# Two-block transformer kernel, odd layer: where the query and key norms and rotations are computed

## The chip, the cores and the metric

The kernel runs on one core of one Trainium2 chip. The metric is the device time in microseconds from one launch to its end; lower is better. The kernel before takes 3747.55 us, the median of 3 runs (3745.74 to 3749.96).

## The reference, cut to what matters

Two blocks of two layers each work on one sequence of 512 tokens with 1024 features, in float32. The change lies in the second layer of the second block (the odd layer). Its mixer is grouped-query attention with 16 query heads, 4 key heads and 64 features a head; every head of queries and keys is normed and then rotated.

```python
def odd_mixer(x, w_in, gqa_q_norm, gqa_k_norm, cos_c, sin_c):
    b, s, _ = x.shape
    g = GQA_HEADS // GQA_KV_HEADS
    q, k, v = _split(x @ w_in, ODD_SPLITS)          # 1024, 256, 256 columns
    q = rms_norm(q.reshape(b, s, GQA_HEADS, GQA_HEAD_DIM), gqa_q_norm)
    k = rms_norm(k.reshape(b, s, GQA_KV_HEADS, GQA_HEAD_DIM), gqa_k_norm)
    v = v.reshape(b, s, GQA_KV_HEADS, GQA_HEAD_DIM)
    q = apply_rope(q, cos_c[:, None, :], sin_c[:, None, :]).reshape(b, s, GQA_KV_HEADS, g, GQA_HEAD_DIM)
    k = apply_rope(k, cos_c[:, None, :], sin_c[:, None, :])
    scale = GQA_HEAD_DIM ** -0.5
    def block(qb):
        sc = jnp.einsum('bqkgd,bskd->bkgqs', qb, k) * scale
        pr = jax.nn.softmax(sc.astype(jnp.float32), axis=-1).astype(v.dtype)
        return jnp.einsum('bkgqs,bskd->bqkgd', pr, v)
```

`rms_norm` divides by the root of the mean square of a head's 64 features (plus 1e-6) and multiplies by a gain per feature. `apply_rope` turns feature j of a head together with feature j + 32.

## The kernel before, in words

The program is a row of stages. `stage` opens a block in which each engine runs its own instruction list; it ends in a barrier of all engines (`all_engine_barrier`, L109). Inside a stage the engines are tied by semaphores alone.

`gemm` (L192) is the stage for all projections. Weights come in tiles of 1 MB through a ring of four slots in SBUF, loaded by SP's queue (L244). Every tile is split into a high part (ScalarE, L321) and a low part (VectorE, L353), two tiles deep, and every output is a row of three products per 128 features (L305): 24 matmuls for an output of 512 columns. Output k lands in PSUM bank k modulo `banks` (8 unless given) and is evacuated by ScalarE (`a`) or VectorE (`v`); output k waits until output k - banks is evacuated. The activations themselves are transposed and split at the start (`lead`, L274, L333, L367). With `side` (made by `beside`) a stage carries other work: `side.pe[k]`, `side.act[k]` and `side.dve[k]` are run by those engines just before output k in their own order, and `sp_after[n]` by SP after the load of tile n. Everything is in order on each engine: work that waits holds what is queued behind it. `prepare_beside` (L1093) is such a side for the first block's layers; its rotations swap halves by small transfers from SBUF to SBUF (L1131, L1132), multiply by the cosine on GpSimd (L1160), by the sine on VectorE (L1140) and add on VectorE (L1145).

`odd_mixer` (L1598) runs four stages. First the projection: four tiles of queries (8 outputs of 128 features, copied to `q`), one of keys (2 outputs; each head is stored twice, so `k` has 4 chunks of 128), one of values (4 outputs); the tables are loaded after the weights (`also`). Then `sums_norm` (L1273): ScalarE squares each of 12 chunks (L1293), TensorE sums the squares per head (L1314), one root and one reciprocal over all 24 heads (L1296, L1301), TensorE spreads the result back over the features (L1321, L1322), VectorE multiplies (L1308). Then `rope` (L807): TensorE swaps halves by a permutation matrix (L819), GpSimd multiplies by the cosine (L826), VectorE multiplies the swapped part by the sine (L837) and adds (L843). Then `attention` (L525).

`attention` works in units of 128 queries of one chunk (two heads) against 512 keys; 8 chunks x 4 units = 32 units. For each unit, in a pipeline some units deep: TensorE's scores (L607), VectorE's maximum of both heads, negated (L748), ScalarE's exponentials with their sums (L690), VectorE's reciprocal of the sums (L756), GpSimd's multiplication of the probabilities (L739), TensorE's transposes (L624), the copy to SBUF by ScalarE (L701) or VectorE (L766), and TensorE's product with the values (L642). The last unit of a chunk closes it: ScalarE (L707) and VectorE (L772) take the output out of PSUM in two parts, and the next chunk's first product waits for that. VectorE's order in a step is: closing, maximum of this unit, reciprocal of the one before, copy of the third before. `attention` serves two other layers too.

## Time and profile before

| what | value |
|---|---|
| median of 3 runs | 3747.55 us |
| profiled execution, its own time | 3756.65 us |
| its span from the first to the last instruction | 3754.8 us |
| TensorE busy with matmuls | 3329.8 us (89%) |
| VectorE / ScalarE / GpSimd busy | 1294.7 / 976.5 / 401.7 us |
| mean granted TensorE clock | 0.943 |

The profile is of one execution. Busy time is the time in which an engine had an instruction under way; the granted clock is a share of TensorE's full speed (1.0 is 2.4 GHz, 0.5 is 1.2 GHz). PE is TensorE, PEld its weight loads, DVE VectorE, ACT ScalarE, POOL GpSimd, SP the engine that issues the transfers; a q behind a name means the queue or sequencer of that engine. The durations of matmuls overlap, since they are pipelined: the step from start to start tells what one costs in a row of them.

### The profile page before, as it was taken

What the parts mean: (1) busy time and instruction counts of PE and PEld (TensorE: products, weight loads), DVE (VectorE), ACT (ScalarE), POOL (GpSimd) and SP (SyncE); (2) the same over time, 40 slices, a digit from 0 to 9 for tenths busy, and PEclk for the clock granted to TensorE, in tenths of its full rate; (3) what the DMA queues carried; (4) which work ended last, traced back from release to release, by engine and by line L of the source; (5) the groups of instructions that cost most, each with busy time, mean ns of one, the idle gap of its engine ahead of it and who ended that gap; (6) DMA issues with size and microseconds to landing.
All of it is one profiled execution on the core that took longest, in us unless ns stands there. A gap on an engine that the chain in (4) does not pass through costs nothing. (4 is left out here: it accounts for less than half of the span.)

```text
span 3754.8 us, 42733 instructions
## 1 busy us (share of the span) xinstructions
PE 3329.8 (89%) x17174; PEld 2288.9 (61%) x17174; DVE 1294.7 (34%) x1709; ACT 976.5 (26%) x1557; POOL 401.7 (11%) x403
## 2 busy tenths in 40 slices
PE   7999899998999899999756769999988787999996
PEld 6875587877876487787644367444436346644442
DVE  4324543333523444242344543111113644311112
ACT  4225333222324414231221431000013343100001
POOL 1005100000104300000000610000000561000000
PEclk9999999999998999999977989999998898999998
DMA  5410223333320014331300123999982101499996
GB/s 154 124 45 1 68 81 99 90 90 80 106 90 23 12 56 135 90 93 42 101 7 14 45 80 120 416 424 424 424 341 80 45 23 58 195 420 424 424 423 289
DMA packets 286517, 587.41 MB, mean 156 GB/s; under 512 B 34666, under 2 KB 228408, under 8 KB 237200
## 3 DMA queue, kind: packets, MB, share of 16 engines
q1 hardware_dynamic: 286352, 585.11, 41.9%
q8 instruction: 115, 1.88, 0.2%
q14 instruction: 50, 0.41, 0.0%
HBM read 581.92 MB, written 2.10 MB: 156 GB/s over the span
## 5 line engine op out<-in xcount | busy, mean ns | idle before, releaser
L2010 PE MATMUL ps<-w_ring,xe 128*64 128x512 f32 x1024 | 232.7, 597 | 6.7 <-PEq L109 5.0
L305 PE MATMUL ps<-h_hi,in_w_hi 128*128 128x512 f32 (+1 forms) x528 | 210.1, 398 | 12.8 <-DVE in_w_lo L353 8.2
L305 PE MATMUL ps<-u_hi,mlp_w_hi 128*128 128x512 f32 x512 | 202.3, 395 | 12.0 <-DVE u_lo L976 12.0
L305 PE MATMUL ps<-h_lo,in_w_hi 128*128 128x512 f32 (+1 forms) x528 | 208.4, 395 | 0.0
L305 PE MATMUL ps<-h_hi,in_w_lo 128*128 128x512 f32 (+1 forms) x528 | 207.8, 394 | 0.0
L353 DVE TENSOR_TENSOR mlp_w_lo<-w_ring,mlp_w_hi 128x2048 fp32r<-128x2048 f32 x64 | 146.7, 2292 | 176.9 <-ACT mlp_w_hi L321 176.9
L305 PE MATMUL ps<-h_hi,mlp_w_hi 128*128 128x512 f32 x512 | 199.3, 389 | 3.0 <-DVE h_lo L367 3.0
L305 PE MATMUL ps<-u_lo,mlp_w_hi 128*128 128x512 f32 x512 | 201.4, 393 | 0.0
L305 PE MATMUL ps<-u_hi,mlp_w_lo 128*128 128x512 f32 x512 | 201.1, 393 | 0.0
L305 PE MATMUL ps<-h_lo,mlp_w_hi 128*128 128x512 f32 x512 | 199.2, 389 | 0.0
L305 PE MATMUL ps<-h_hi,mlp_w_lo 128*128 128x512 f32 x512 | 199.2, 389 | 0.0
L2010 PEld LDWEIGHTS ps<-w_ring,xe 128*64 128x64 f32 x1024 | 71.6, 137 | 136.8 <-issue 136.5
L321 ACT ACTIVATE mlp_w_hi<-w_ring 128x2048 fp32r<-128x2048 f32 x64 | 122.1, 1908 | 113.4 <-PE ps L305 113.4
L2088 DVE SCALAR_TENSOR_TENSOR ye_lo<-ps,g_now,ye_hi 128x1024 fp32r<-128x1024 f32 x16 | 20.5, 1284 | 355.0 <-ACT ye_hi L2055 355.0
L2068 DVE TENSOR_TENSOR x<-x,ps 128x512 f32<-128x512 f32 x128 | 82.9, 685 | 173.6 <-PE ps L1973 173.2
L353 DVE TENSOR_TENSOR in_w_lo<-w_ring,in_w_hi 128x2048 fp32r<-128x2048 f32 (+2 forms) x48 | 89.2, 1858 | 141.8 <-ACT in_w_hi L321 141.6
L2010 PE MATMUL ps<-ex_back,xe 128*64 128x512 f32 x512 | 116.9, 597 | 21.4 <-DMA ex_back<-in_w 21.4
L690 ACT ACTIVATE w_ring<-ps,at_top 128x128 f32<-128x128 f32 (+1 forms) x192 | 99.5, 523 | 126.5 <-DVE at_top L748 126.2
L2010 PE MATMUL ps<-ex_front,xe 128*64 128x512 f32 x512 | 116.9, 597 | 15.7 <-DMA ex_front<-in_w 15.5
L1846 PE MATMUL ps<-sel_now,xs_hi 128*128 128x128 f32 x512 | 123.8, 284 | 0.0
L1846 PE MATMUL ps<-sel_now,xs_lo 128*128 128x128 f32 x512 | 122.8, 282 | 0.0
L305 PEld LDWEIGHTS ps<-h_hi,in_w_hi 128*128 128x128 f32 (+1 forms) x528 | 99.5, 188 | 37.6 <-DVE in_w_lo L353 15.2
(513 smaller groups left out, 7176.0 us busy)
## 6 DMA issues: line engine op xcount, KB each, us to landing
w_ring<-in_w SPq DMA_DIRECT2D x192, 1024.0 KB, 12.8
ex_front<-in_w SPq DMA_DIRECT2D x96, 1024.0 KB, 13.3
ex_back<-in_w SPq DMA_DIRECT2D x96, 1024.0 KB, 13.5
w_ring<-in_w_in SPq DMA_DIRECT2D x32, 1024.0 KB, 6.4
w_ring<-in_w_up SPq DMA_DIRECT2D x32, 1024.0 KB, 5.8
w_ring<-in_w_down SPq DMA_DIRECT2D x32, 1024.0 KB, 5.7
w_ring<-in_cmp_w SPq DMA_DIRECT2D x16, 512.0 KB, 4.2
w_ring<-in_w_out SPq DMA_DIRECT2D x8, 1024.0 KB, 6.4
```

The source lines that it names most:

```text
L305: mm = pe.matmul(ps[0:o.rows, k % banks, 0:o.cols], lhsT, rhs, start=(j == 0), stop=(j == len(o.mm) - 1))
L321: act.activation(w.hi[:, n % SPLITS, 0:used], ring.slots[:, n % RING, 0:used], ACT.Copy).then_inc(s.hi_done, 1)
L353: dve.tensor_tensor(w.lo[:, n % SPLITS, 0:used], ring.slots[:, n % RING, 0:used], w.hi[:, n % SPLITS, 0:used].bitcast(F32), ALU.subtract). ...
L690: act.activation(probs[:, u % (LAG + 1), a, 0:n], ps[:, S_BANK + 2 * (u % 2) + a, 0:n], ACT.Exp, bias=top[:, u % 8, a:a + 1], accum_out=to ...
L1846: mm = pe.matmul(ps[:, bank + j // 4, j % 4 * P:j % 4 * P + P], part[:, t, pairs_of(j)], E.sel_now[:, t, :], start=(t == 0 and part is xs. ...
L2010: mm = pe.matmul(ps[rows, bank + half, :], lhsT, slot(2 * m + a)[:, kk, 512 * half:512 * half + 512], start=(k == 0), stop=(k == DC - 1))
L2068: dve.tensor_tensor(d, d, ps[:, TR_BANK + n % 2, :], ALU.add).then_inc(s.added, 1)
L2088: dve.scalar_tensor_tensor(ye.lo[:, :], ps[:, Y_BANK:Y_BANK + 2, :].rearrange("p b n -> p (b n)"), g_now[:, :], ye.hi[:, :].bitcast(F32), ...
```

## The change

The stages `sums_norm` and `rope` of the odd layer are gone; a side, `heads_beside`, carries their work in the projection stage.

- The key tile comes first (outputs 0 and 1), then the four query tiles (2 to 9), then the values (10 to 13). `banks` is 4 (`HEAD_BANKS`); banks 4 to 7 serve the side.
- Query norms: ScalarE squares each query chunk from PSUM as its evacuation, VectorE writes the chunk times the gain. TensorE sums the squares of each head with the tokens on the partitions: `sq` is the stationary operand and two columns of ones move, 4 matmuls a chunk. After a root and a reciprocal the result `rq` (which carries the 1/8 of the attention's scale) is not multiplied into the queries: it is the column by which ScalarE's exponential scales the scores (`sharp`). The negated maximum is multiplied by the same column, by a new VectorE instruction behind the maximum with a wait on VectorE's own semaphore `peaked`. For the other attentions `sharp` is None and nothing is added.
- Key norms: squares on ScalarE, sums on TensorE in two parts (before outputs 3 and 4), root, reciprocal, four transposes (before output 5), split in high and low part, spread back by TensorE in two parts (before 6 and 7), multiplied by VectorE in two parts.
- Rotations: halves are swapped by transfers from SBUF to SBUF issued by SP after the last weight load, four for each chunk with 32 partitions each, in the order queries 0-1, 2-3, keys 0-1, queries 4-5, keys 2-3, queries 6-7. Cosine, sine and sum are all on VectorE. The sine table carries the sign.
- The tables are loaded after weight tile 1, before tiles 2 to 5.

```diff
-                    for a in range(2):
-                        act.activation(probs[...], ps[...], ACT.Exp,
-                                       bias=top[:, u % 8, a:a + 1], accum_out=total[:, u % 8, a:a + 1]).then_inc(s.exped, 1)
+                                       bias=top[:, u % 8, a:a + 1], accum_out=total[:, u % 8, a:a + 1],
+                                       scale=groups[g].sharp(i)[:, a:a + 1] if groups[g].sharp else 1.0).then_inc(s.exped, 1)
...
-                    dve.tensor_reduce(top[:, u % 8, :], ps[:, b:b + 2, 0:keys(i)], AX.X, ALU.max, negate=True).then_inc(s.maxed, 1)
+                    peak = dve.tensor_reduce(top[:, u % 8, :], ps[:, b:b + 2, 0:keys(i)], AX.X, ALU.max, negate=True)
+                    if groups[g].sharp:
+                        peak.then_inc(s.peaked, 1)
+                        dve.wait_ge(s.peaked, u + 1)
+                        peak = dve.tensor_tensor(top[:, u % 8, :], top[:, u % 8, :], groups[g].sharp(i), ALU.mult)
+                    peak.then_inc(s.maxed, 1)
...
-                gemm(nc, "oi", ps, ring, tiles, lead=flips(C, lambda i, j: x[:, i, j * P:(j + 1) * P], h), also=tables)
-        with ExitStack() as c2:
-            chunks = [q[:, j, :] for j in range(8)] + [k[:, j, :] for j in range(4)]
-            sums_norm(nc, "on", ps, C, [(c, gains[:, (n >= 8):(n >= 8) + 1]) for n, c in enumerate(chunks)], add, back[:, :, :])
-            rope(nc, "ro", ps, [(c, cos, sin) for c in chunks], perm)
+                gemm(nc, "oi", ps, ring, tiles, lead=flips(C, lambda i, j: x[:, i, j * P:(j + 1) * P], h), side=side, banks=HEAD_BANKS)
...
+def heads_beside(nc, ctx, ps, C, I, q, k, rq):
...
+    turning = [(q[:, 0:2, :], 0), (q[:, 2:4, :], 1), (k[:, 0:2, :], None), (q[:, 4:6, :], 2), (k[:, 2:4, :], None), (q[:, 6:8, :], 3)]
...
+    def query(c):
+        def a(e, p, st):
+            if c >= 4:
+                e.wait_ge(st.s.n_summed, 1 + (c - 4) // 2 + 1)
+            elif c == 0:
+                e.wait_ge(st.s.n_summed, 1)
+            return e.activation(sq[:, c % 4, :], p, ACT.Square)
+        def v(e, p, st):
+            return e.tensor_scalar(q[:, c, :], p, gains[:, 0:1], None, ALU.mult)
...
+    def swaps(sp, s):
+        for n, (x, g) in enumerate(turning):
+            if g is not None:
+                sp.wait_ge(s.evac_v, s.done_v[Q_OUT + 2 * g + 1])
+            for m in range(x.shape[1]):
+                c = before[n] + m
+                if g is None:
+                    sp.wait_ge(s.n_scaled, m + 1 if n == 2 else m + 3)
+                if c >= 4:
+                    sp.wait_ge(s.n_added, c - 3)
+                for b in (0, 64):
+                    sp.dma_start(tmp[b:b + 32, c % 4, :], x[b + 32:b + 64, m, :]).then_inc(s[f"n_swap{n}"], 16)
+                    sp.dma_start(tmp[b + 32:b + 64, c % 4, :], x[b:b + 32, m, :]).then_inc(s[f"n_swap{n}"], 16)
...
+    def sum_queries(g):
+        def go(pe, s):
+            pe.wait_ge(s.evac_a, s.done_a[Q_OUT + 2 * g + 1])
...
+            for m in (2 * g, 2 * g + 1):
+                for i in range(TT):
+                    mm = pe.matmul(q_sums[g % 2][:, i, 2 * m:2 * m + 2], sq[:, m % 4, i * P:(i + 1) * P], ones[:, 0:2], start=True, stop=True)
+            mm.then_inc(s.n_summed, 1)
...
+    def rotate(n):
...
+            dve.wait_ge(s[f"n_swap{n}"], 64 * len(chunks))
+            for m, c in enumerate(chunks):
+                dve.tensor_tensor(x[:, m, :], x[:, m, :], cos[:, :], ALU.mult).then_inc(s.n_cosined, 1)
+                dve.tensor_tensor(tmp[:, c % 4, :], tmp[:, c % 4, :], sin[:, :], ALU.mult).then_inc(s.n_sined, 1)
+            for m, c in enumerate(chunks):
+                dve.wait_ge(s.n_cosined, c + 1)
+                dve.wait_ge(s.n_sined, c + 1)
+                dve.tensor_tensor(x[:, m, :], x[:, m, :], tmp[:, c % 4, :], ALU.add).then_inc(s.n_added, 1)
...
+    side = beside(names, sp,
+                  {3: sum_keys(0), 4: sum_keys(2), 5: flip_keys, 6: then(spread_keys(0), sum_queries(0)), 7: spread_keys(2), 8: sum_queries(1),
+                   9: sum_queries(2), V_OUT + 1: sum_queries(3)},
+                  {2: square_keys, 4: root_keys, 5: split_hi, 7: root_queries(0), 9: root_queries(1), V_OUT: root_queries(2), V_OUT + 2: root_queries(3)},
+                  {2: tables_in, 4: invert_keys, 5: then(split_lo, rotate(0)), 6: scale_keys(0), 7: then(scale_keys(2), rotate(1)),
+                   8: then(invert_queries(0), rotate(2)), 9: then(invert_queries(1), rotate(3)), V_OUT: then(invert_queries(2), rotate(4)),
+                   V_OUT + 2: rotate(5), V_OUT + 3: invert_queries(3)},
+                  pool, {1: load_tables, 5: swaps})
```

## Rows read from the trace of the kernel before

**Rows 1.** Busy time by stretch: sum (instructions) per engine, clock, DMA share, GB/s

```profile
2840.00:2909.00 69.00, 68.80 (x336) 58.45 (x336) 21.44 (x22) 15.74 (x17) 0.00 (x0) 0.96 0.19 59
2909.00:2938.00 29.00, 21.09 (x48) 10.06 (x48) 13.66 (x16) 9.07 (x14) 0.00 (x0) 0.76 0.00 0
2938.00:2962.00 24.00, 13.50 (x24) 5.56 (x24) 19.94 (x24) 0.00 (x0) 18.89 (x12) 0.71 0.00 1
2962.00:3083.00 121.00, 104.75 (x512) 45.85 (x512) 65.09 (x88) 67.70 (x154) 98.92 (x64) 0.94 0.11 35
...
2962.00:2972.00 10.00, 8.49 (x21) 3.27 (x22) 4.69 (x6) 5.50 (x13) 4.31 (x3) 0.50 0.89 288
```

**Rows 2.** Time line at the stage borders: start, duration (us), engine, line, operation

```profile
2908.84 0.42 DVE L402 TENSOR_SCALAR ov<-ps 128x256 f32<-128x256 f32 x1 [5.33 <-PE ps L305]
...
2910.11 2.19 ACT L1293 ACTIVATE on_sq<-oq 128x512 f32<-128x512 f32 x4 [3.77 <-PEq L109]
...
2962.42 3.78 PE L607 MATMUL ps<-ok,oq 64*128 64x512 f32 x8 [10.23 <-PEq L109]
```

**Rows 3.** Time line of ScalarE inside the projection

```profile
2870.13 0.60 ACT L401 ACTIVATE oq<-ps 128x512 f32<-128x512 f32 x1 [3.46 <-PE ps L305]
2875.63 1.92 ACT L321 ACTIVATE oi_w_hi<-w_ring 128x2048 fp32r<-128x2048 f32 x1 [4.90 <-PE ps L305]
2881.01 0.60 ACT L401 ACTIVATE oq<-ps 128x512 f32<-128x512 f32 x1 [3.46 <-PE ps L305]
```

**Rows 4.** Narrow matmuls of another stage, time line; and a weight load's group

```profile
1068.48 0.55 PE L1189 MATMUL ps<-n_tables,w2k 128*128 128x62 f32 x4
1068.96 0.63 PE L1193 MATMUL ps<-w2v,n_tables 128*31 128x64 f32 x8
1069.53 0.50 PE L305 MATMUL ps<-h_hi,in_w_hi 128*128 128x512 f32 x1
1069.86 0.40 PE L305 MATMUL ps<-h_lo,in_w_hi 128*128 128x512 f32 x1
...
L305 PEld LDWEIGHTS ps<-h_hi,in_w_hi 128*128 128x128 f32 (+1 forms) x528 | 99.5, 188 | 37.6 <-DVE in_w_lo L353 15.2
```

**Rows 5.** VectorE's groups by line: busy us, mean ns, idle before

```profile
L1140 DVE TENSOR_TENSOR gate_a<-gate_a 128x512 f32<-128x512 f32 x16 | 10.3, 684 | 0.0
L1308 DVE SCALAR_TENSOR_TENSOR oq<-oq,gqa_g,ps 128x512 f32<-128x512 f32 x8 | 6.0, 747 | 2.1 <-PE ps L1322 1.3
```

**Rows 6.** Transfers issued by SP, and GpSimd's first use of such a swap

```profile
942.25 0.62 SPq L1131 DMA_DIRECT2D gate_a<-qb  x1
942.92 0.62 SPq L1132 DMA_DIRECT2D gate_a<-qb  x1
...
944.93 1.29 POOL L1160 TENSOR_TENSOR qb<-qb,gate_a 128x512 f32<-128x512 f32 x1 [2.49 <-DMA gate_a<-qb]
...
2852.20 0.43 SPq L248 DMA_DIRECT2D sin<-in_c_sin  x1
```

**Rows 7.** VectorE and GpSimd side by side; one line's duration min/median/max (ns)

```profile
L1232 DVE TENSOR_TENSOR gate_b<-kvc,cpos x16: 565/578/1616, 83.6 to 975.5; 128x248 f32<-128x248 f32 x16
...
967.86 2.29 DVE L353 TENSOR_TENSOR in_w_lo<-w_ring,in_w_hi 128x2048 fp32r<-128x2048 f32 x1 [0.54 <-ACT in_w_hi L321]
...
968.15 4.62 POOL L1160 TENSOR_TENSOR kwd<-kwd,gate_a 128x512 f32<-128x512 f32 x2 [3.61 <-DMA gate_a<-kwd]
```

**Rows 8.** The attention: a wait (total us, times, longest), and GpSimd's time line

```profile
PE ps L642 <- DVE mixT_lo L772: 8.1, 7, 2.0
...
2967.64 46.37 POOL L739 TENSOR_SCALAR gqa_probs<-gqa_probs,gqa_inv 128x512 f32<-128x512 f32 x30 [7.06 <-DVE gqa_inv L756]
```

**Rows 9.** Time line of the attention at the close of a chunk

```profile
3006.63 0.16 DVE L756 RECIPROCAL gqa_inv<-gqa_total 128x2 f32<-128x2 f32 x1
...
3007.40 1.13 PE L607 MATMUL ps<-ok,oq 64*128 64x512 f32 x4
...
3007.51 1.23 DVE L766 COPY gqa_probsT<-ps 128x1024 f32<-128x1024 f32 x1 [0.72 <-PE ps L624]
...
3008.71 0.69 DVE L772 TENSOR_TENSOR mixT_lo<-ps,mixT_hi 128x512 fp32r<-128x512 f32 x1
```

More of the change, by code:

```diff
@@ L1602, in sb @@
             return c.enter_context(nc.sbuf_tensor(name, shape, F32))
-        gains, add, back = sb("gqa_g", [P, 2]), sb("add3", [P, 12, 24]), sb("back3", [24, 12, P])
-        perm, cos, sin = sb("perm3", [P, P]), sb("cos3", [P, T]), sb("sin3", [P, T])
-        gn = [I[n][0].rearrange("(d a) -> d a", a=1) for n in ("gqa_q_norm_2", "gqa_k_norm_2")]
-        tables = ([(gains[64 * m:64 * m + 64, n:n + 1], gn[n]) for m in range(2) for n in range(2)]
-                  + [(add[:, :, :], I["c_add3"]), (back[:, :, :], I["c_back3"]), (perm[:, :], I["c_perm3"]), (cos[:, :], I["c_cos3"]),
-                     (sin[:, :], I["c_sin3"])])
-        q, k, v = sb("oq", [P, 8, T]), sb("ok", [P, 4, T]), sb("ov", [P, TT, 256])
+        q, k, v, rq = sb("oq", [P, 8, T]), sb("ok", [P, 4, T]), sb("ov", [P, TT, 256]), sb("orq", [P, TT, 16])
         with ExitStack() as c2:
             h = pair(nc, c2, "xT_o", [P, DC, T])
-            tiles = [tile(DC, 256, lambda slot, n=n: [(slot, W(w_in, DC, 256 * n, 256))],
-                          lambda w, n=n: [fm(w, h, 128 * j, P, range(DC), **to(q[:, 2 * n + j, :], "AV"[j])) for j in range(2)])
-                     for n in range(4)]
+            side = heads_beside(nc, c2, ps, C, I, q, k, rq)
             def both(dst):
@@ L1624, in both @@
                 return dict(a=a, v=v)
-            tiles.append(tile(DC, 256, lambda slot: [(slot, W(w_in, DC, 1024, 256))],
-                              lambda w: [fm(w, h, 128 * j, P, range(DC), **both(k[:, 2 * j:2 * j + 2, :])) for j in range(2)]))
+            tiles = [tile(DC, 256, lambda slot: [(slot, W(w_in, DC, 1024, 256))],
+                          lambda w: [fm(w, h, 128 * j, P, range(DC), **both(k[:, 2 * j:2 * j + 2, :])) for j in range(2)])]
+            tiles += [tile(DC, 256, lambda slot, n=n: [(slot, W(w_in, DC, 256 * n, 256))],
+                           lambda w, n=n: [fm(w, h, 128 * j, P, range(DC), **side.query(2 * n + j)) for j in range(2)])
+                      for n in range(4)]
             tiles.append(tile(DC, 256, lambda slot: [(slot, W(w_in, DC, 1280, 256))],
@@ L1638, in odd_mixer @@
         groups = [Names(chunk=c, qk=lambda a, c=c: (q[rows(a), c, :], k[rows(a), c // 2, :]),
-                        v=lambda a, kb, c=c: v[:, kb, HD * (c // 2):HD * (c // 2) + HD], bias=None, gate=None, cmp=None) for c in range(8)]
+                        v=lambda a, kb, c=c: v[:, kb, HD * (c // 2):HD * (c // 2) + HD], bias=None, gate=None, cmp=None,
+                        sharp=lambda i, c=c: rq[:, i, 2 * c:2 * c + 2]) for c in range(8)]
         attention(nc, "gqa", ps, C, groups, "full", mixT, ring, nxt)
+HEAD_BANKS = 4
@@ L2229, in constants @@
         c[f"c_cos{n}"], c[f"c_sin{n}"], c[f"c_perm{n}"] = cos[rows], sin[rows], swap(size, starts, rot // 2)
-    for n, row_of in ((2, [(0, 0, 256), (0, 0, 256), (1, 1, 128)]), (3, [(2 * j, 2 * j + 1, HD) for j in range(12)])):
+    c["c_sin3"] = np.where((q % 64 < 32)[:, None], -c["c_sin3"], c["c_sin3"])
+    c["c_add3"] = np.stack([q < HD, q >= HD, np.full(P, HD * EPS), 0 * q], 1)
+    c["c_back3"] = np.stack([np.stack([(q // HD == r % 2) & (m == r // 2) for m in range(4)]) for r in range(8)])
+    for n, row_of in ((2, [(0, 0, 256), (0, 0, 256), (1, 1, 128)]),):
         m = max(b for _, b, _ in row_of) + 1
@@ L2236, in constants @@
             add[HD:P, j, b] = 1.0 / width
-        scale = np.array([HD ** -0.5 if n == 3 and j < 8 else 1.0 for j in range(len(row_of))])
-        c[f"c_add{n}"], c[f"c_back{n}"] = add, (add > 0).transpose(2, 1, 0) * scale[None, :, None]
+        c[f"c_add{n}"], c[f"c_back{n}"] = add, (add > 0).transpose(2, 1, 0)
     c["c_zero"] = np.zeros((GRANK, 256))
```

112 lines of the change are left out of this document (108 added, 4 removed).

## The prediction

> **What bounds the kernel now.** I read the stretches first, then the time line where stages meet, then the waits of the attention. The odd layer's query-key preparation is a row of stages on one path: projection (2840 to 2909 us), norms (2909 to 2938), rotations (2938 to 2962), attention (2962 to 3083) [rows 1]. Each ends in a barrier of all engines. In the projection TensorE is busy without a gap (68.8 of 69 us) at 0.96 of its clock, that is nearly all at 2.4 GHz, while VectorE works 21.4 us, ScalarE 15.7 and GpSimd not at all. In the next two stages TensorE's clock is 0.76 and 0.71, and one short operation waits for another. From the last copy of the projection (ends 2909.26) to the attention's first matmul (2962.42) 53.2 us pass, and nothing else of the program runs in them [rows 2]. In the attention GpSimd is busy 98.9 us and TensorE 104.7 of 121, so two engines bound it together.
>
> **What goes.** Both stages go: 53.2 us. One barrier stays; the first work of the norms starts 0.85 us after the projection's last copy [rows 2], so 53.2 - 0.85 = 52.3 us are won. What they did is now done beside the projection, or in the exponentials.
>
> **What TensorE gets in the projection.** It is the engine without a gap, so each of its new instructions counts. An output of 24 matmuls takes (2881.01 - 2870.13) / 2 = 5.44 us, 0.227 us each [rows 3].
> - Sums of squares: 12 chunks x 4 matmuls (128x128 stationary, 2 columns moving), each two instructions in this type, so 96. No row has 2 columns in this type. The nearest has 62 columns: four such start in 1068.96 - 1068.48 = 0.48 us, 0.12 each [rows 4]. From below: eight with a narrow stationary and 64 columns take 0.57 us, 0.07 each; from above: one weight load of 128x128 lasts 0.19 us [rows 4]. I take 0.12, as the weights, not the columns, fill it: 96 x 0.12 = 11.5 us (6.7 to 18.2).
> - Four transposes, 4 x 0.12 = 0.5; eight spreading matmuls with 512 columns, 8 x 0.227 = 1.8.
> - Eight changes from one kind to another, an estimate of 0.1 each (the first projection matmul after such a group takes 0.33 us, 1069.53 to 1069.86, instead of 0.227 [rows 4]): 0.8.
>
> **Does TensorE wait?** I laid the new orders side by side, output by output, with the durations of the rows. Output 1 ends three outputs before 2870.1, at 2853.8. ScalarE then has two copies (1.2 us), a weight split (1.9 [rows 3]), a small copy (0.6) and the first two squares (1.2) to do: 2858.8. TensorE reaches the first key sums at 2859.2. The second half of the sums ends at 2868.4, the roots follow on ScalarE behind a weight split (1.9 us), the inversion on VectorE behind its own (2.3 us [rows 7]), at 2874.3; TensorE wants to transpose at 2873.8: 0.5 us of waiting. That is the price of cutting the key work in two parts with outputs between them. Outputs 4 to 13 wait for the evacuation four outputs back (four banks, not eight); it is 10 us old in each case. ScalarE's squares of the queries replace copies of the same size; its square of output 2 waits for the key sums until 2868.6, with only output 3 queued behind.
> Sum: 11.5 + 0.5 + 1.8 + 0.8 + 0.5 = 15.1 us more, the projection's matmuls end near 2924.
>
> **VectorE beside it.** 36 rotation steps at 0.684 us (GpSimd does nothing here, so the clean rows hold), overlapping to 0.6: 22 to 25 us; four scalings of keys at 0.75: 3.0 [rows 5]; four more evacuations at 0.69, like the subtraction from PSUM [rows 9]: 2.8; small ones 1.5. With 21.4 that is 51 to 54 of 84 us: hidden, but in order. A rotation waits for its swap on VectorE, and an evacuation and a weight split queue behind it. The first swap can start when output 3 is evacuated (2870.6). Eight transfers are issued at 0.67 us each, and the first use came 1.4 us after the last issue ended (942.92 + 0.62 to 944.93) [rows 6]; I add a microsecond as these carry four times the bytes: about 8 us a pair. So VectorE waits at 2876 to 2879 with output 5 and split 4 behind it; that split is wanted at 2897 and done at 2886. SP has 48 swaps, 32 us, behind all weight loads; eight small tables now stand before loads 2 to 5; issued in 0.4 to 0.7 us each [rows 6] they delay them by some 5 us, while split 2 is first done at 2855. The last pair can start when output 9 is evacuated (2911), lands at 2919, is turned by 2922.7: just inside the end of the matmuls. I take 0.4 us for the last evacuation behind it. This is the thinnest cover of the change; a microsecond more per pair would show one for one.
> Up to here: -52.3 + 15.1 + 0.4 = -36.8 us.
>
> **What the attention gets.** Each of 32 units gets one more VectorE instruction, a product of two small tiles in SBUF, between the maximum and the exponentials, with a wait on VectorE itself. By the reciprocal of the same size it takes 0.16 us [rows 9], and about 0.04 for the wait. Behind it stand the inverses that GpSimd waits for, the transposed copy and the closing subtraction. Clean, that is 0.2 us a unit, nearly all beside TensorE, as VectorE is busy 65 of 121 us.
> But it reads two inputs from SBUF beside a GpSimd that never rests (30 instructions in 46.37 us, 1.55 each [rows 8]). What that does is in the trace: a VectorE product of two SBUF inputs took 1616 ns instead of 578 when it met a GpSimd product, and two GpSimd products of 1.29 us each took 4.62 where they met VectorE's 2.29 us split [rows 6, 7]. One waits for the other's end. The Trainium skill (SBUF - State Buffer, Who interferes with whom) has the same as a rule: the shared port is locked for a whole instruction, and a VectorE operation with two SBUF inputs is among those that want it; read strictly, each of the 32 products would wait for a whole remaining instruction. The trace agrees (578 to 1616 ns); the sum below goes by the rows.
> The wait found by a product that arrives at random: half of 1.55 at most, about 0.5 to 0.8. It counts where TensorE waits for VectorE, which is at the close of a chunk: 8.1 us over 7 times for the closing subtraction [rows 8]. There VectorE idles only from 3006.79 to 3007.51 before the copy [rows 9]; a product of 0.2 + 0.8 eats the 0.7 and pushes 0.3 to 0.4 on, seven times: 2.8 us. Elsewhere a unit has an instruction of slack; I add 1.0. The exponentials may lengthen by their second column operand; ScalarE is busy 67.7 of 121 us, so even a tenth more hides.
> On the other side TensorE comes into the attention from full work. Now it starts at half clock (0.50 in the first 10 us [rows 1]), eight scoring instructions take 3.78 us, four at full clock 1.13 [rows 2, 9]: the first unit is 0.8 us earlier. Together 2.8 + 1.0 - 0.8 = +3.0. From below 0.2 x 7 - 0.8, about +0.5; from above, if each product waits 1.3 us, VectorE's own work in a chunk of four units is 4 x (1.22 + 0.2 + 1.3 + 0.16) + 2 x 1.22 + 0.69 = 14.6 us against a chunk of 13.5 now: +1.1 x 8, with some closings +12.
>
> **Sum.** -36.8 + 3.0 = -33.8 us. On the profiled execution (3756.65 us, span 3754.8) that gives 3722.9. That execution lies 9.1 us over the median of the runs shown, and the change is in a stretch both have: 3747.55 - 33.8 = 3713.8 us.
>
> **Rivals.**
> - The small products are not held by GpSimd (they are 2 columns, the rows that show the wait have 248 and more): attention +0.5, 3747.55 - 36.8 + 0.5 = 3711.3 us.
> - They are held nearly a whole instruction each and VectorE bounds the attention: +12, 3722.8 us. For it: GpSimd's instructions stand back to back, so a product nearly always meets one. Against: VectorE idles 56 of 121 us.
> - SP bounds the projection. If a swap of 32 partitions takes 1.33 us to issue instead of the 0.67 of 8 partitions, five pairs from 2883.4 take 53 us, and with landing and rotation the stage ends near 2943 instead of 2923: 3713.8 + 20 = 3733.8 us. Against: a table of 128 partitions is issued in 0.43 us [rows 6].
> - Slower than before: the attention's product is passed over, GpSimd's next instruction taking the port again each time. From (52.3 - 15.5) / 32 = 1.15 us a unit on, the whole gain is gone. If each waited for two instructions, 3.1 us, VectorE would need 2.3 + 0.2 + 3.1 = 5.6 us a unit against 3.4: +70, 3781 us. Against: in the rows that show the wait it was one instruction's rest (1616 - 578 = 1.04 us of 1.29).
> - The change doesn't do what it says: a wait in the new orders holds TensorE several microseconds at each of the eight places, or the clock falls behind the narrow matmuls, and the two removed stages come back inside the projection: 52 us at most, 3748 to 3750 us.
>
> **Chances.** Forecast 0.45; not held 0.26; held long 0.13; SP 0.08; slower 0.04; not as it says 0.04. Range 3702 to 3733 us: below, the sums at 0.07 us and a free product (-5 and -2.5, and some for the earlier full clock); above, sums at 0.19 with held products, or most of the SP case. A change is told from none by 0.2%, 7.5 us. Faster 0.93, within 0.03, slower 0.04.
>
> **What would show it.** The stretch from the projection's first matmul to the attention's first is 122.6 us now and should be 86. The 2-column matmuls start 0.12 us apart. TensorE stands once, for about 0.5 us, before the transposes of the key norms. The last rotation ends within a microsecond of the last matmul. The new product shows a median duration well over 0.2 us, and the closings hold TensorE 10 to 11 us instead of 8.1. The prediction is wrong if the attention takes more than 6 us longer, if TensorE waits for VectorE or a swap in the projection by more than 2 us, or if the removed stretch is given back after the attention.

## The result, and the profile after

The changed kernel takes 3719.74 us (median of 4 runs, 3713.41 to 3724.55); the kernel before, on the same chip, 3748.09 (4 runs, 3745.74 to 3749.96). The ratio is 0.9912, with a 95% interval of 0.9895 to 0.9929: 26.6 to 39.4 us faster. The two medians lie 28.4 us apart; the ratio's centre is 33.0 us. The forecast was 3713.8 us, and 33.8 us faster.

The profiled execution after took 3716.64 us, its span 3714.8; TensorE was busy 3304.4 us (89%), GpSimd 382.0, at a mean granted clock of 0.947. Its odd layer in four stretches of busy time (columns as in [rows 1]): the projection; the attention's first 10.8 us; the rest of it; what follows.

```profile
2835.90:2921.70 85.80, 85.25 (x444) 72.01 (x444) 50.54 (x72) 21.93 (x32) 0.00 (x0) 0.94 0.30 85
2921.70:2932.50 10.80, 7.22 (x26) 3.25 (x28) 6.03 (x12) 6.83 (x16) 5.41 (x4) 0.84 0.87 277
2932.50:3043.40 110.90, 95.50 (x488) 42.49 (x484) 64.76 (x109) 65.33 (x140) 93.67 (x61) 0.98 0.04 12
3043.40:3200.00 156.60, 127.53 (x921) 115.08 (x922) 69.30 (x98) 47.44 (x65) 11.62 (x8) 0.89 0.24 85
```

Where four stages stood [rows 1], two are left, and the attention follows the projection. VectorE is busy 50.5 us in the projection instead of 21.4, TensorE has no gap in either. The count, in this pair of executions:

| from .. to | before | after | difference |
|---|---|---|---|
| projection's first matmul to attention's first | 2839.90 to 2962.42: 122.5 | 2835.93 to 2922.54: 86.6 | -35.9 |
| attention's first matmul to the last closing subtraction's end | to 3081.07: 118.65 | to 3043.41: 120.87 | +2.2 |
| all before the projection | 2839.90 | 2835.93 | -4.0 |
| all behind the attention | 673.7 | 671.4 | -2.3 |

The last two lines are no effect of the change: behind the attention it is 670.7 to 677.0 us in the executions of the experiments. Of the first, 0.8 us is chance too: the projection starts at half clock each time, before for 13 matmuls and after for 9, 0.2 us each. In the executions profiled below the projection's first matmul stands anywhere from 2825 to 2846 us, in kernels that differ only behind it; that scatter is most of the spread of the total times, so the experiments are read by stretches. Two of these serve for it: the **period of a chunk** in the attention (from one closing subtraction to the next; the first five of the seven intervals of an execution agree within 0.02 us; the last two, where the attention runs out, are shorter: 11.03 and 5.2 or 6.7 to 6.9 us in most), and the stretch between the two first matmuls, which lies within 83.4 to 86.6 us in the executions that keep the changed kernel's projection.

The length of the whole attention is not steady. In the seven profiled executions whose attention has both additions and the late closing (the changed kernel and experiments 1, 2, 7, 8, 9 and 10) it is 119.6 to 123.2 us, with the same period in all. The difference goes with the falls of TensorE's clock:

```profile
2962.42:2970.90 8.48, 7.39 (x16) 2.24 (x16) 3.82 (x5) 4.37 (x10) 3.21 (x3) 0.50 0.91 294
3074.40:3078.40 4.00, 3.99 (x12) 1.40 (x14) 0.00 (x0) 0.00 (x0) 0.00 (x0) 0.58 0.00 0
```

```profile
2922.54:2928.00 5.46, 3.12 (x12) 1.05 (x12) 2.85 (x5) 4.08 (x8) 0.91 (x1) 1.00 0.81 261
2928.60:2931.40 2.80, 2.77 (x10) 1.21 (x9) 2.01 (x4) 1.63 (x4) 2.80 (x3) 0.51 1.10 349
2938.60:2942.20 3.60, 3.60 (x14) 1.93 (x16) 1.59 (x4) 1.69 (x4) 3.60 (x3) 0.54 0.00 0
```

Before the change (the first two lines) it is half at the attention's start and once near its end; after (the other three) the attention starts at full clock, TensorE works 3.1 of the first 5.5 us, and then the clock is half twice. From the first scores to the end of the first closing it takes 33.5 or 33.6 us in the executions with one such fall or none, 34.7 to 35.4 in those with two or with one of double length; the last interval takes 5.2 us, with a fall near the end 6.7 to 6.9. So the +2.2 of this pair is in part chance: 1.2 too much at the start, 1.65 too little at the end. The steady part of the difference is five intervals at 0.52 us: 2.6.

Time line of TensorE and VectorE in the projection after the change (start, duration, engine, line):

```profile
2861.38 1.84 PE L1718 MATMUL ps<-add,on_sq 128*128 128x2 f32 x16
...
2868.44 0.40 PE L305 MATMUL ps<-xT_o_hi,oi_w_lo 128*128 128x512 f32 x1
...
2868.87 0.60 PE L1761 MATMUL ps<-ident,on_rk 128*8 128x128 f32 x4
...
2873.12 0.69 DVE L1797 TENSOR_TENSOR oq<-oq,cos 128x512 f32<-128x512 f32 x1 [2.27 <-DMA on_tmp<-oq]
...
2918.43 1.29 DVE L1802 TENSOR_TENSOR oq<-oq,on_tmp 128x512 f32<-128x512 f32 x2
...
2921.25 0.42 DVE L402 TENSOR_SCALAR ov<-ps 128x256 f32<-128x256 f32 x1 [1.37 <-PE ps L305]
```

Sixteen two-column instructions hold TensorE 1.70 us, from the first one's start to the start of the next projection matmul: 0.106 each. TensorE comes late to the key transposes by some 0.2 us. VectorE waits 2.27 us for the first swap, which nobody feels, and has the last rotation done at 2919.7, 1.5 us ahead of the last matmul's end and two ahead of the last value copy's.

One stretch of the trace was not foreseen. TensorE, in the order of time, behind the transposes:

```profile
2875.71 0.39 PE L1780 MATMUL ps<-on_rs_lo,back_r 8*128 8x512 f32 x1
2876.03 2.33 PE L1734 MATMUL ps<-add,on_sq 128*128 128x2 f32 x16
2878.22 0.77 PE L305 MATMUL ps<-xT_o_hi,oi_w_hi 128*128 128x512 f32 x1
2878.79 0.63 PE L305 MATMUL ps<-xT_o_lo,oi_w_hi 128*128 128x512 f32 x1
2879.21 0.63 PE L305 MATMUL ps<-xT_o_hi,oi_w_lo 128*128 128x512 f32 x1
...
2884.31 0.39 PE L305 MATMUL ps<-xT_o_hi,oi_w_lo 128*128 128x512 f32 x1
2884.54 0.39 PE L305 MATMUL ps<-xT_o_hi,oi_w_hi 128*128 128x512 f32 x1
```

From 2878 to 2884 the matmuls start 0.43 us apart instead of 0.23: the granted clock is 0.50, 1.2 GHz, though TensorE has not stood. Ahead of it lie four spreading matmuls with 8 rows and sixteen with 2 columns, in a row. Fourteen matmuls at 0.2 us more make 2.8 us, the last of the sums, already slowed (2.33 for 1.84), a little more.

In the attention one closing repeats every 13.98 us (before: 13.46), in the first five intervals. After the change, TensorE's wait there (total us, times, longest):

```profile
PE ps L642 <- DVE mixT_lo L778: 10.4, 7, 2.0
```

The new product's group (busy us, mean ns):

```profile
L753 DVE TENSOR_TENSOR gqa_top<-gqa_top,orq 128x2 f32<-128x2 f32 x32 | 5.2, 163 | 1.1
```

And the close of a chunk in the time line:

```profile
2982.25 0.16 DVE L753 TENSOR_TENSOR gqa_top<-gqa_top,orq 128x2 f32<-128x2 f32 x1
2982.33 0.17 DVE L762 RECIPROCAL gqa_inv<-gqa_total 128x2 f32<-128x2 f32 x1
2982.44 0.78 ACT L690 ACTIVATE gqa_probs<-ps,gqa_top,orq 128x512 f32<-128x512 f32 x1 [0.70 <-DVE gqa_top L753]
...
2983.22 0.77 ACT L690 ACTIVATE gqa_probs<-ps,gqa_top,orq 128x512 f32<-128x512 f32 x1
...
2983.97 0.59 ACT L708 ACTIVATE mixT_hi<-ps 128x512 fp32r<-128x512 f32 x1
2984.59 0.69 DVE L778 TENSOR_TENSOR mixT_lo<-ps,mixT_hi 128x512 fp32r<-128x512 f32 x1 [0.36 <-ACT mixT_hi L708]
...
2985.43 1.08 PE L642 MATMUL ps<-gqa_probsT,ov 128*64 128x512 f32 x4 [1.40 <-DVE mixT_lo L778]
```

The same product with the values in the kernel before:

```profile
3009.55 1.08 PE L642 MATMUL ps<-gqa_probsT,ov 128*64 128x512 f32 x4 [1.02 <-DVE mixT_lo L772]
```

The product takes 163 ns in the mean: as a rule it is not held beside GpSimd. (Of 352 such products in the eleven profiled executions that have them, ten took more than 0.20 us, the longest 0.69; what held those few is open.) The exponentials take 0.77 us each (0.68 to 0.69 before). And the rows show a chain from VectorE's maximum to TensorE: product, exponential, exponential, the output's copy, its subtraction, TensorE's next product with the values, each starting where the one before ends. TensorE stands 1.40 us at its end; before the change it was 1.02.

### The profile page after: what moved, and what is told of

The parts are those of the page before. It is cut to its first block and busy times, and to the rows that moved or that the text cites. A ratio compares the mean times of both kernels' runs of the same rounds, so it can differ in the third digit from the quotient of the medians.

```text
span 3714.8 us, 42845 instructions
## 1 busy us (share of the span) xinstructions
PE 3304.4 (89%) x17210; PEld 2282.9 (61%) x17210; DVE 1295.3 (35%) x1752; ACT 979.0 (26%) x1558; POOL 382.0 (10%) x391
## 6 DMA issues: line engine op xcount, KB each, us to landing
w_ring<-in_w SPq DMA_DIRECT2D x192, 1024.0 KB, 12.4
ex_back<-in_w SPq DMA_DIRECT2D x96, 1024.0 KB, 13.4
```

## Experiments

Twelve kernels ran, in three groups, each group on one chip (1 to 4; 5, 6, 8 and 10; 7, 9, 11 and 12). The kernel before took 3750.12, 3752.43 and 3755.14 us there, and each ratio is to the kernel before on the same chip.

**1. The changed kernel again.**

> The changed kernel itself, unaltered, as the anchor of this group. Both theories: 3719 us within 5 (0.991 of before); the projection stretch (first projection matmul to the attention's first) 86.6 us within 0.5, the attention from its first matmul to its last closing subtraction 120.9. If the drop of TensorE's clock at 2877 us of the profile is a chance event of one execution, it is absent or elsewhere here; if it belongs to the kernel's order of work it comes back at the same output.

3719.04 us (6 runs, 3714.56 to 3721.5), ratio 0.9912 [0.9894, 0.9930]: the result holds on another chip. Stretch 85.80 us, period 13.98, attention 119.66, which is 1.2 us less than the 120.9 expected, by one fall of the clock in it instead of two. In the projection the clock falls at the same output, behind the first query sums, for seven matmuls this time instead of fourteen. So it seems to belong to the order of the work, and its length varies.

**2. The first query sums apart from the spreading.**

```
-  5: flip_keys, 6: then(spread_keys(0), sum_queries(0)), ...
+  5: then(sum_queries(0), flip_keys), 6: spread_keys(0), ...
```

> The first query sums move from before output 6 to before output 5, ahead of the transposes of the key norms; all work stays. Theory A: the drop to half clock (matmuls 0.427 us apart instead of 0.228 over some 13 of them, about 3 us) comes from the spreading matmuls with 8 rows and the 2-column sums standing together; apart, no matmul of the projection is 0.43 us apart, the stretch takes 83.5 us instead of 86.6 and the time is about 3 us (0.1%) lower. Rival B: the clock falls by the load of the whole stretch; then it falls at some other place for as long, the stretch keeps 86.6 us and the time is the same.

Stretch 84.15 us, that is 1.65 and 2.5 less than in the two executions of the changed kernel. Less 0.2 us for each matmul that the stage starts with at half clock (11 here, 12 and 9 there) it is 82.0 against 83.4 and 84.8, and less 0.2 for each of the 7 and 14 matmuls of the fall these too come to 82.0: the fall is all the difference. The granted clock is 1.00 in every 2 us from 2868 to 2898, and the only matmuls 0.43 us apart are the stage's first. The time, 3718.73 us (3710.59 to 3728.77, ratio 0.9909), can't show two microseconds. The fall is not strict in the kernels that keep the old order: among nine profiled executions that have it (the changed kernel and experiments 1, 3 to 7, 10 and 11) seven fell, for 7 to 14 matmuls, and two did not (stretches 83.4 and 83.7). With the sums apart (here and in experiment 12), none of two. Theory A is favoured, by 2.5 us at most, not proved by so few: if two in nine escape by chance, two in a row come once in twenty.

**3 to 5. The attention's two additions, one by one and both out.** The edits leave the product out (3), the scale operand (4), both (5); in all three the queries' scale is set to ones.

```
-  peak.then_inc(s.peaked, 1)                                                                   (3, 5)
-  dve.wait_ge(s.peaked, u + 1)                                                                 (3, 5)
-  peak = dve.tensor_tensor(top[:, u % 8, :], top[:, u % 8, :], groups[g].sharp(i), ALU.mult)   (3, 5)
-  scale=groups[g].sharp(i)[:, a:a + 1] if groups[g].sharp else 1.0      (4, 5)
+  scale=1.0
-  dve.reciprocal(rq[...], rq[...])          (3, 4, 5)
+  dve.tensor_scalar(rq[...], rq[...], 0.0, 1.0, ALU.mult, ALU.add)
```

> Left out of the computation: the queries' norm scale (it is set to 1), and with it the product of the maximum and that scale in each unit of the odd layer's attention. The exponentials keep their second column operand. Theory A (product 0.16 us, never held, but on the path at each closing; the second column adds 0.09 to each of two exponentials on the same path): the chunk period falls from 13.98 to about 13.7 us, the attention by 1.5 to 2 us. Rival B (the product is off the path, the loss is the exponentials' alone): 13.9 to 14.0. Rival C (it is the product alone): 13.46 as before the change, the attention 4 us shorter.

> Left out of the computation: the queries' norm scale (it is set to 1), and with it the scale operand of the exponentials of the odd layer's attention. The product of the maximum stays. Theory A (both are on the path at each closing, 0.18 us from two exponentials): chunk period from 13.98 to about 13.75 us, exponentials 683 ns instead of 773. Rival B (ScalarE's idle third hides it, as the prediction said): 13.9 to 14.0. Rival C (the column alone is the loss): 13.46.

> Left out of the computation: the queries' norm scale, with the product of the maximum and the scale operand of the exponentials in the odd layer's attention. Each alone took 0.33 us off the chunk period of 13.98. Theory A (one closing chain, maximum, product, two exponentials, output copies; something else stands at 13.46 as before the change): 13.46 us, the attention as long as before the change less the full clock at its start, 117 to 117.5 us counted from its first matmul. Rival B (the two add up freely): 13.98 - 0.34 - 0.33 = 13.31 us.

| | period of a chunk | TensorE's wait for the closing, 7 times | exponential |
|---|---|---|---|
| changed kernel | 13.98 | 10.4 us | 773 ns |
| no product | 13.64 | 9.2 | 774 |
| no second column | 13.66 | 9.3 | 684 |
| neither | 13.45 | 8.1 | 683 |
| before the change | 13.46 | 8.1 | 683 |

One execution of each (3712.06, 3705.61, 3725.04 us; the last had a late start of the projection, at 2845), read by their periods, which the rest of the program doesn't touch. From neither, the second column adds 0.19 and the product 0.21, by the exponentials' 2 x 0.09 and the product's 0.16 with its wait. Both together add 0.53, 0.13 more than the sum. The time lines show where: in the chunk's third unit the transposes start 1.19 us behind the start of the product with the values in the changed kernel, and 1.01 before the change, without the product, without the column and without both.

```profile
2977.63 1.08 PE L642 MATMUL ps<-gqa_probsT,ov 128*64 128x512 f32 x4
2977.70 1.02 ACT L702 ACTIVATE gqa_probsT<-ps 128x1024 f32<-128x1024 f32 x1
2978.82 1.06 PE L624 MATMUL ps<-ident,gqa_probs 128*128 128x128 f32 x8
```

The transposes start 0.1 us behind the end of ScalarE's copy (2977.70 + 1.02), which stands behind the two exponentials. That this copy is what they wait for is read from the time line, not tried by itself. Of the three theories A holds, B and C fall; only its period for 4 was a little high (13.75).

**6. A wide product beside GpSimd.**

```
+  dve.tensor_tensor(wide[:, 0, :], wide[:, 1, :], wide[:, 2, :], ALU.mult)   # 128x512, each unit
```

> Added on VectorE in each unit of the odd layer's attention, right behind the small product: one product of two SBUF tiles of 128x512, which nobody reads. Theory A (a product of two SBUF inputs is held by GpSimd's multiplication only if it is wide, while 2 columns pass in 0.163 us): the wide one takes 0.68 us clean and 1.0 to 1.7 where a GpSimd instruction is under way, or GpSimd's own grows from 1.566; the 2-column one stays at 0.16. Rival B (this GpSimd instruction, one tensor and a column, never holds VectorE, whatever the width; only GpSimd products of two tensors do): the wide one takes 0.66 to 0.70 in all units and GpSimd's stays at 1.566.

The view of single lines (ns: min/median/max), VectorE's wide and narrow products and GpSimd's multiplication:

```profile
L759 DVE TENSOR_TENSOR gqa_wide<-gqa_wide x32: 678/684/685, 2928.5 to 3032.0; 128x512 f32<-128x512 f32 x32
L756 DVE TENSOR_TENSOR gqa_top<-gqa_top,orq x32: 160/161/283, 2928.4 to 3031.9; 128x2 f32<-128x2 f32 x32
L741 POOL TENSOR_SCALAR gqa_probs<-gqa_probs,gqa_inv x64: 1557/1562/1990, 2931.3 to 3037.4; 128x512 f32<-128x512 f32 x64
```

Not one of 32 wide products is held, and 25 of them ran beside a GpSimd instruction, which is busy 99.8 us here. GpSimd's median stays too; six of its 64 took 1.60 to 1.99 us, where in the changed kernel none took more than 1.58. The period is 13.98: even 0.68 us more of VectorE in each unit costs nothing in the steady chunks. Rival B holds but for those six, and A falls: it isn't the width. One execution, 3721.8 us.

**7. The cosine products back on GpSimd.**

```
-  dve.tensor_tensor(x[:, m, :], x[:, m, :], cos[:, :], ALU.mult).then_inc(s.n_cosined, 1)
+  pool.tensor_tensor(x[:, m, :], x[:, m, :], cos[:, :], ALU.mult).then_inc(s.n_cosined, 1)   # behind the swap
```

> The cosine products of the rotations (12 of 128x512) go to GpSimd, beside the projection, as the stage before the change had them; the sine products and the additions stay on VectorE. Theory A (two products of tensors hold each other on the two engines: one instruction's rest each): VectorE's sine products take 1.2 to 1.6 us instead of 0.68 where they meet, GpSimd's 1.3 to 1.7, the last rotation ends up to 1.5 us later and the stretch from first projection matmul to the attention's first is 0 to 2 us longer than 85.8. Rival B (no holding, as with the wide product beside the multiplication by a column): sine products stay at 0.68, VectorE is 8 us freer, the stretch within 0.5.

```profile
2895.88 2.98 POOL L1815 TENSOR_TENSOR oq<-oq,cos 128x512 f32<-128x512 f32 x2 [6.34 <-DMA on_tmp<-oq]
...
2896.32 3.09 DVE L1797 TENSOR_TENSOR on_tmp<-on_tmp,sin 128x512 f32<-128x512 f32 x2
```

Here the two hold each other, seen in the time line above: VectorE's two sine products take 3.09 us instead of 1.3 while GpSimd's cosine products run. Of the twelve sine products five are held, at 1.38 to 1.79 us, and seven take 0.63 to 0.69 (mean 1093 ns instead of 682); GpSimd's take 1.27 to 1.31 alone and 1.72 to 1.80 where they meet VectorE. The stretch is 83.67 us, in an execution without the fall of the clock, and the time 3716.76 us (4 runs, 3712.85 to 3720.97; ratio 0.9902 [0.9886, 0.9917]): the same as the changed kernel's 0.9912 on another chip within the intervals. Theory A holds, though the stretch is no longer for it. So holding is real where GpSimd multiplies two tensors, and absent, but for the few cases named above, where it multiplies one by a column; and **rotations on VectorE alone** gain nothing that these runs can tell, since both ways are hidden.

**8. The sums twice.** Each two-column instruction is issued twice, in the queries' sums as shown and in the keys' alike.

```
+  for _ in range(2):
       mm = pe.matmul(q_sums[...][:, i, 2*m:2*m+2], sq[:, m % 4, i*P:(i+1)*P], ones[:, 0:2], start=True, stop=True)
```

> Each of the 96 two-column instructions of the sums of squares is done twice. Theory A (TensorE has no slack in the projection, and each costs 0.106 us): the stretch from the projection's first matmul to the attention's first grows from 85.8 to 86.6 us by 96 x 0.106 = 10.2, and by more where the clock drops: a drop behind the doubled spreading-and-sums place lasts longer, and the doubled groups alone, 3.4 us of 2 columns, could bring drops of their own, 3 us each; so 96 to 108 us, time +10 to +20. Rival B (part of it hides in waits of TensorE): under +8.

Stretch 106.0 us: 19.4 to 20.2 more than the changed kernel's. 96 x 0.106 = 10.2 is the sums; nearly all of the rest is the clock. Behind five of the six doubled groups it falls, in stretches of busy time of the same columns:

```profile
2868.90:2872.20 3.30, 3.30 (x10) 2.65 (x10) 0.00 (x0) 0.00 (x0) 0.00 (x0) 0.50 0.00 0
2880.00:2885.70 5.70, 5.70 (x15) 4.54 (x15) 3.81 (x4) 3.06 (x4) 0.00 (x0) 0.50 0.14 36
2899.70:2903.00 3.30, 3.30 (x9) 2.55 (x9) 0.94 (x2) 0.00 (x0) 0.00 (x0) 0.50 0.42 107
2916.60:2920.00 3.40, 3.40 (x11) 2.72 (x11) 3.40 (x6) 0.00 (x0) 0.00 (x0) 0.52 0.43 109
2927.70:2933.80 6.10, 6.10 (x16) 4.85 (x16) 1.47 (x3) 0.00 (x0) 0.00 (x0) 0.50 0.01 3
```

TensorE is busy all through these, at half clock. 48 matmuls at 0.2 us more are 9.6; against the 82.0 + 2.4 us of a stretch without a fall and with this one's cold start (12 matmuls), 106.0 is 21.6 more, of which 10.2 + 9.6 = 19.8 are these two and part of the rest the sums themselves, slowed at half clock (4.10 and 4.03 us for 32 instead of 3.63). The median is 3740.93 us (10 runs, 3727.13 to 3752.33; ratio 0.9962 [0.9948, 0.9977]); the wide spread fits falls whose lengths vary, of which only one execution was profiled. Theory A holds: nothing of the sums hides, and they bring falls of their own.

**9. All key norms in one place.** `6: then(spread_keys(0), then(spread_keys(2), sum_queries(0)))`.

> All four key norms are spread in one place, before output 6, instead of two before output 6 and two before output 7; the second pair of spreading products waits for VectorE's scaling of the first pair, which frees its banks. Theory A (the two parts are what keeps TensorE from waiting): VectorE does that scaling 5 us later, behind a rotation, an evacuation and a weight split, so TensorE stands 4 to 6 us there and its clock falls behind the stand for 5 us or more; the stretch grows from 85.8 to 90 to 94 us. Rival B: the time of the second place is saved, and TensorE's wait is under 1.5 us: 85 to 87 us.

```profile
2880.62 0.39 PE L1780 MATMUL ps<-on_rs_lo,back_r 8*128 8x512 f32 x1
2886.12 0.76 PE L1779 MATMUL ps<-on_rs_hi,back_r 8*128 8x512 f32 x1 [5.10 <-DVE ok L1787]
...
2888.09 3.57 PE L1734 MATMUL ps<-add,on_sq 128*128 128x2 f32 x16
```

TensorE stands 5.10 us for VectorE's scaling, and its clock is at half for the spreads, the sums (3.57 us instead of 1.84) and eleven matmuls more. Stretch 94.09 us, just above Theory A's 90 to 94; time 3731.35 (4 runs, 3729.04 to 3734.99; ratio 0.9940 [0.9925, 0.9955]). In the stretch 8 us are given back, by the ratios some 10. Spreading the keys in two parts is worth that.

**10. GpSimd's multiplication at half the time.**

```
-  pool.tensor_scalar(p, p, inv[:, u % 8, a:a + 1], None, ALU.mult)
+  pool.tensor_scalar(p, p, inv[:, u % 8, a:a + 1], 1.0, ALU.mult, ALU.mult)
```

> GpSimd's multiplication of the probabilities by a column gets a second scalar step, times 1.0, in all three attentions without a gate. Before the change the gated form with two steps took 775 ns for 128x512 where the form with one took 1565. Theory A (the form with one step is slow by its form, and GpSimd is one of two bounds): 775 ns each, chunk period of the odd layer from 13.98 to between 12.6 and 13.4 us, where TensorE's 3.09 us a unit and the closings bound it; the attention 5 to 9 us shorter, the other two 2 to 6 us together, time 3707 to 3713. Rival B (the closing chain alone sets the period): GpSimd's instruction halves, but the period stays within 0.1 of 13.98. Rival C (the second step isn't what halves it): 1566 ns still.

```profile
L740 POOL TENSOR_SCALAR gqa_probs<-gqa_probs,gqa_inv x64: 691/692/700, 2914.8 to 3019.1; 128x512 f32<-128x512 f32 x64
```

692 ns instead of 1566 (667 instead of 1541 from start to start), by a second step that does nothing. And the period stays at 13.98, TensorE's wait for the closings at 10.4 us, the time at 3719.11 (6 runs, 3705.18 to 3725.19; ratio 0.9914 [0.9896, 0.9933]). GpSimd, busy 82% of the attention [rows 1], bounds nothing here. Rival B holds; A, with its 12.6 to 13.4 us, and C fall.

**11. The closing one step earlier.**

```
 ScalarE, VectorE:
-  u = step - LAG - 2 - (TT - 1)
-  if u >= 0 and u % TT == TT - 1:
+  u = step - LAG - 1 - (TT - 1)
+  if 0 <= u < nu and u % TT == TT - 1:
 VectorE: keep(u // TT) now behind inverses(step - 1), not ahead of peaks(step)
```

> In all attentions the closing of a chunk (ScalarE's copy of the output, VectorE's subtraction) moves one step earlier in both engines' orders: on ScalarE ahead of the step's two exponentials, on VectorE behind the inverses and ahead of the transposed copy. Theory A (the odd layer's chunk period is set by the closing chain: maximum, product, two exponentials, copy, subtraction, then TensorE's next product with the values): TensorE's wait of 1.40 us at each closing goes, and the period falls from 13.98 to 12.5 to 12.9, where GpSimd's 8 x 1.566 = 12.5 or TensorE's 4 x 3.09 = 12.4 bounds it; the attention 7 to 10 us shorter, all attentions together 8 to 18 us. Rival B: the copy ahead of the exponentials delays them and the same wait comes back at the exponentials: period 13.5 to 13.98.

3691.6 us (5 runs, 3684.43 to 3697.59), ratio 0.9829 [0.9814, 0.9844]: 28 us below the changed kernel's median, 31 by the ratios, and the intervals are far apart. Period 13.10, the odd layer's attention 114.96 us instead of 119.6 to 123.2. The same closing in the time line of this kernel:

```profile
2971.91 0.60 ACT L708 ACTIVATE mixT_hi<-ps 128x512 fp32r<-128x512 f32 x1 [0.25 <-PE ps L642]
...
2972.41 0.77 ACT L690 ACTIVATE gqa_probs<-ps,gqa_top,orq 128x512 f32<-128x512 f32 x1
...
2972.54 0.69 DVE L778 TENSOR_TENSOR mixT_lo<-ps,mixT_hi 128x512 fp32r<-128x512 f32 x1
2972.82 1.13 PE L607 MATMUL ps<-ok,oq 64*128 64x512 f32 x4
2973.15 1.21 DVE L772 COPY gqa_probsT<-ps 128x1024 f32<-128x1024 f32 x1
...
2974.47 1.08 PE L642 MATMUL ps<-gqa_probsT,ov 128*64 128x512 f32 x4 [0.52 <-issue]
```

The output's copy now starts as the matmuls it waits for end (ScalarE stands 0.25 us for them), and TensorE scores the next unit beside copy and subtraction. Theory A in its mechanism, not in its sizes: the period is 0.2 above its range and the odd layer's attention is 5 to 8 us shorter (7 to 10 expected), while the whole gain is above its 8 to 18. In the odd layer 0.52 us of the stall stay: TensorE's product starts at 2974.47, 0.1 us behind the end of VectorE's transposed copy (2973.15 + 1.21), which the subtraction now pushes back. `attention` runs three other times in this program, with 48, 48 and 16 units, and the edit reaches them all. The larger part of the gain lies in the two with 48, those of the gated layers: from the first maximum of the one to the last of the other it is 1010.3 us, in the two executions of the changed kernel 1024.5 and 1027.7. That the same chain closes their chunks is not shown. The copy and the subtraction were moved together; which of the two does it was not tried.

**12. All three together.** The edits of 2, 10 and 11.

> The early closing, GpSimd's multiplication with a second step (692 ns instead of 1566) and the first query sums apart from the spreading. Theory A: with the closing out of the way GpSimd's 12.5 us a chunk is the next bound or shares it, so the second step now pays 0 to 0.3 us a chunk on the odd layer (12.4 to 12.6), and more where the chunks are short of TensorE work; time 2 to 8 us below the early closing alone, 3695 to 3710. Rival B: TensorE is the only bound left and GpSimd's half gives nothing here either: equal to the early closing within 2 us, less the 2 us of the clock.

3687.76 us (5 runs, 3684.15 to 3693.51), ratio 0.9823 [0.9809, 0.9836]. Period 13.10 again, not Theory A's 12.4 to 12.6, so with the closing out of the way GpSimd is still no bound on the odd layer: rival B. (Its 8 x 1.566 = 12.5 us a chunk lay below 13.10 before.) The stretch is 84.14 us, 2.5 below the early closing's 86.63, with no fall of the clock. The medians differ by 3.8 us with overlapping runs; that it beats the early closing alone is not shown, that it beats both kernels is.

## Why the prediction was right, and where it was not

**What goes, and what TensorE gets.** -36.8 us forecast between the two first matmuls, -35.9 measured (-36.7 in the repetition). From the projection's first matmul to its last copy's end: 69.4 us before, 85.7 after, +16.4 against 15.1 + 0.4 = +15.5. Its terms: the sums 10.2 for 11.5, a little less than taken and nothing of it hidden (experiment 8); the barrier 0.85 as forecast; the wait before the key transposes 0.2 for 0.5; the last copy's 0.4 not there. Missing from the sum was the fall of the clock, 1.4 to 2.8 us. The prediction named such a fall only in the rival "doesn't do what it says", as a catastrophe at every place; it is one place and small. Without falls and without the half clock at the start the stretch grows by 14.3 us (83.3 - 2.2 in experiment 2 against 69.4 - 2.6 before). Sums too dear by 1.3 and a fall left out made the right size together, which is luck.

**Covers.** They held. Rotations on VectorE ended 1.5 us ahead of the last matmul, a little earlier than the order laid out said (its sign was "within a microsecond"); SP bound nothing (the swaps were issued some 0.6 us apart, for 0.67 taken). The prediction named 0.5 us of waiting as the price of cutting the key work in two parts; experiment 9, with the spreading in one part, shows that cutting it saves 8 us there.

**The attention: the right sum from two wrong steps.** +3.0 forecast, +2.2 measured in one pair, +1.0 with the repetition, +2.6 in its steady part; TensorE waits 10.4 us at the closings, within the forecast's 10 to 11. That this came out is luck. The wait for GpSimd, "about 0.5 to 0.8" us for each product, failed: the product takes 0.163 us at a GpSimd that is busy 82% of the time, and a 256 times wider one is not held either (experiment 6). And "ScalarE is busy 67.7 of 121 us, so even a tenth more hides" failed: the tenth stands at the closing, in series, twice. The prediction reckoned 0.3 to 0.4 us per closing for the holding; the runs show 0.38 there, of 0.20 product and 0.18 exponentials, and another 0.15 in the chunk's third unit. The rival "not held" had the mechanism of the product right, and its 0.2 us a closing with it (0.21 a chunk, experiments 3 to 5), but its sum wrong (+0.5), since it too put the exponentials at nothing. It lay 2.5 us below the forecast; the measured times can't tell the two apart, the durations and periods do.

Where did the wrong rule come from? [rows 6, 7] show VectorE held beside GpSimd, and all of them are GpSimd operations on two tensors (L1160). (The 4.62 us there are not the split's doing alone: 3.15 us beside the split, then 1.51 beside a VectorE product of two tensors.) The attention's multiplies one tensor by a column. Experiments 6 and 7 set the two cases side by side: 684 ns beside the one, 1380 to 1790 beside the other. The Trainium skill (SBUF - State Buffer, Who interferes with whom) says that a VectorE instruction with two SBUF inputs contends with a GpSimd instruction that reads SBUF; in this kernel it does with one kind of reader and not with the other, and the measurement decides.

**"Two engines bound it together."** Wrong for GpSimd: at 44% of its time per instruction nothing moved (experiment 10), nor behind the mended closing (12). It was taken from busy shares. What sets the period is TensorE's 3.09 us a unit, 12.4 a chunk, plus the stand at the closing; the profile before already showed it, as 8.1 us waited for the closing subtraction [rows 8].

**Full clock at the start.** The granted clock of the first 10.8 us is 0.84, for 0.50 before [rows 1]; GpSimd's first instruction comes 4.55 us behind the first scores instead of 5.22: 0.67 won for 0.8 forecast. The clock does not stay: in eleven of the thirteen executions profiled after the change it falls to 0.50 from 4.5 to 6.2 us into the attention, where TensorE had stood for part of the time before. What the start is worth shows best in experiment 5, whose period is that of before: its first closing ends 32.4 us behind the first scores instead of 33.5.

## What to carry to other kernels

A busy share doesn't show what bounds a stage: ask which wait recurs with its period, and follow the chain back from it; on that chain a 2-column instruction and 90 ns more of a half-idle engine count in full, and closing a chunk one step earlier (a copy and a subtraction), in the attentions of all four layers, gave about as much as removing two stages. When a helper operation is taken from one engine's queue to another's, look at its place in the order, not at the engine's total. A contention seen in one row holds for that pair of operations; before it is carried to another pair, the other pair has to be seen.

## What was not expected of the hardware

- GpSimd's multiplication of 128x512 by a column takes 1566 ns; with a second scalar step (times 1.0) 692 ns (experiment 10).
- VectorE's product of two SBUF tiles is slowed by GpSimd's product of two tensors (682 to 1093 ns in the mean, 1.38 to 1.79 us where held) and not by GpSimd's multiplication by a column (678 to 685 ns in all 32).
- The granted clock can fall to 0.50 with TensorE busy all through: behind 32 matmuls of 2 columns in a row in five cases of six (in one of the five four of 8 rows stood ahead of them), behind four of 8 rows and 16 of 2 columns in seven executions of nine, behind 16 alone in none of the executions profiled here.
- A matmul with 2 columns and a 128x128 stationary in this type costs 0.106 us per instruction in a row of 16, though one weight load of 128x128 lasts 0.19 us [rows 4].
